# Three score buffers for the prompt's attention units, a place of its own for each value page set, and loads moved between queues, in a two-layer decoder step

## The chip, the cores and the metric

The kernel runs on one core of a Trainium2 chip. A core has five engines with queues of their own: TensorE (PE in the profile, its weight loads are PEld), VectorE (DVE), ScalarE (ACT), GpSimd (POOL) and SyncE (SP). They wait for each other through semaphores only; SP computes nothing here and issues most DMAs, POOL and ACT issue some. The metric is the device time of one execution in microseconds.

## The reference

One inference step of a decoder with two layers, for 256 prompt rows and 8 sequences of 4 new rows each (288 columns together), model width 1024, all float32. Each layer norms the rows, projects them, runs a token mixer beside a cross-attention into 256 memory tokens, projects back, adds, and runs a SwiGLU channel mixer. Layer 0's mixer is a state-space scan; layer 1's is a sparse attention with three branches, each with its own softmax, gated and summed:

```python
def nsa_sample(h, mem_kv, pool_cmp, pool_slc, win_buf, page_table, w_in, ...):
    q, kv_cmp, kv_slc, kv_win, gates, qm = nsa_split(h @ w_in)
    past_cmp = pool_cmp[page_table]...          # 16 pages of 128 rows per sequence
    o_cmp, p = cmp_attend(q, q_pos, ckv, slopes)
    tok = block_tokens(select_blocks(p, q_pos, total))
    kv_past = pool_slc[pages, tok_past % PAGE_SIZE, hi]
    o_slc = slc_attend(q, q_pos, tok, kv_sel, slopes)
    o_win = win_attend(q, q_pos, kv_w, k_pos, slopes)
```

For the 8 sequences, 16 key pages and 16 value pages each come from a pool by a page table; for the prompt, the same branches are computed from the prompt's own rows, for 12 heads.

## The kernel before

Activations lie with features on the partitions, so a projection is a series of 128x128 weight tiles against 288 columns. Weights pass through three slots of a tile called `slabs` (`SLOTS = 3`, 2048 columns each, 1 MB a slab). SP loads slab n when the slab three before it has been used: `load` (L1967) waits for a semaphore and issues. Every engine's program is written out by hand in one order, and a wait blocks all that stands behind it on that engine's queue. PSUM has 8 banks; `banks.fill`, `take`, `give` are the semaphores by which PE writes a bank, a reader takes it and gives it back.

The work in order, on the profile's time axis: layer 0's memory projection, input projection with the memory attention's steps in between (0 to 91 us), the scan with the compression of the cached pages beside it (to 360), output projection and channel mixer (`channel_mixer`, L719 first half with `in_wfi` slabs, L759 second half with `in_wfo` slabs; to 614); layer 1's memory projection (L517), input projection (L497; to 725), the sparse attention (725 to 934), output projection, channel mixer and stores (to 1247).

Places that the change touches:

- Layer 0's start. VectorE makes the scan's input matrices in two rounds r = 0 and 1 (L1631 to L1637: four products and one sum each) and then does `mem_soft(0, 2)`, `(0, 3)`, `(0, 4)`: the softmax of memory heads 2 and 3 and of the sequences, whose results PE turns (L552, L584). SP loads the cached pages of sequence 0 (16 DMAs, L2003), then the second half of the memory values (L2007), which PE multiplies in L596.
- Layer 0's end and layer 1's start. SP issues the 16 `in_wfo` slabs, then 16 key pages (L398, `load_key_pages(sp, SP, 0, 0)`), then layer 1's memory slabs. After the input projection's slabs it also fills the three slots with the first three slabs of layer 1's output projection.
- The units (L972 to L980 on PE, L1821 to L1826 on VectorE). A unit n is one pair of prompt heads in one branch; there are 12. PE makes its scores (L923), VectorE adds the distances (`unit_max`, L1790, L1794, L1795), ScalarE takes the exponential (L1350), VectorE scales (`unit_prob`, L1806, L1808, L1814), PE transposes (L934), ScalarE copies, PE multiplies with the values (L947, L951, L954). The scores of unit n live in `SU[n % 2]`, so `unit_max(n)` waits until unit n - 2 has been transposed. Beside each unit PE computes one tile of the sequences' scores against a key page chunk (`page_scores`, L968, bank 7 alone) and VectorE evicts it (`page_scores_out`, L1799). Four chunks of key pages (c = 0 to 3, 16 pages on SP and 16 on POOL) serve three units each; two places in `arena` alternate, so chunk c waits for the last page scores of chunk c - 2.
- After the units. Window keys and values are loaded and used (L1008, L1040 first part), the selected-block softmax is made, its weights are transposed 16 times (L1061), and then PE multiplies them with the value pages in four pairs of sequences, 32 matmuls on 16 pages each plus 2 (L1040), in order (0,1), (2,3), (4,5), (6,7). A matmul counts twice in the profile's rows (two passes). The value pages (L405) of even sequences are loaded by SP, of odd ones by POOL, in order, each set of 16 when its place is free: 0 and 1 after the window scores, 2 to 4 after the window values' use, 5 and 6 after the transposes (they lie over the scores in `phase`), 7 after the first pair, into the place of sequence 1:

```python
VSLOT = [b if b < 7 else 1 for b in range(B)]
...
if b < 2:
    for h in range(H):
        banks.take(eng, ("sws", h))
elif b < 5:
    eng.wait_ge(win_used, 1)
elif b < 7:
    banks.take(eng, ("st", NPG))
else:
    eng.wait_ge(pair_used, 1)
```

## Time and profile before

| | |
|---|---|
| median of 3 runs | 1255.3 us (1254.72 to 1261.52) |
| the profiled execution's own time | 1248.54 us |
| its span | 1246.8 us |
| PE busy | 1122.9 us (90%) |
| VectorE, ScalarE, GpSimd busy | 371.2, 203.2, 244.1 us |
| granted TensorE clock, mean | 0.945 |
| bytes moved | 185.13 MB, mean 148 GB/s |

The span is divided into 40 slices of 31 us; PE is at nine tenths or more in most of them, except at the start and in slices 23 to 31 (about 720 to 960 us), the sparse attention, where its busy share and its granted clock are lower. A row of the timeline gives start, duration (us), engine, line, operation, tiles and, in brackets, how long the engine had been idle before and what ended that. A row of the chain gives start, duration and what the end was waiting for then.

### The profile page before, as it was taken

What the parts mean: (1) busy time and instruction counts of PE and PEld (TensorE: products, weight loads), DVE (VectorE), ACT (ScalarE), POOL (GpSimd) and SP (SyncE); (2) the same over time, 40 slices, a digit from 0 to 9 for tenths busy, and PEclk for the clock granted to TensorE, in tenths of its full rate; (3) what the DMA queues carried; (4) which work ended last, traced back from release to release, by engine and by line L of the source; (5) the groups of instructions that cost most, each with busy time, mean ns of one, the idle gap of its engine ahead of it and who ended that gap; (6) DMA issues with size and microseconds to landing.
All of it is one profiled execution on the core that took longest, in us unless ns stands there. A gap on an engine that the chain in (4) does not pass through costs nothing. (4 is left out here: it accounts for less than half of the span.)

```text
span 1246.8 us, 16400 instructions
## 1 busy us (share of the span) xinstructions
PE 1122.9 (90%) x6032; PEld 819.0 (66%) x6032; DVE 371.2 (30%) x789; ACT 203.2 (16%) x497; POOL 244.1 (20%) x314
## 2 busy tenths in 40 slices
PE   6879999999989999999899986675669899999996
PEld 5555666666767777777667773333547677777774
DVE  5709767420141111100222125657200411111002
ACT  3220000002230000100032114443201300000000
POOL 0707666620001111110000201304420011111000
PEclk9979999999989999999999977888879899999998
DMA  8455443331415666654522452554632243333431
GB/s 321 189 174 180 143 127 114 101 103 37 166 65 203 221 236 238 276 172 140 190 110 101 148 165 70 153 203 131 186 90 102 93 144 135 135 135 104 138 132 70
DMA packets 59112, 185.13 MB, mean 148 GB/s; under 512 B 8609, under 2 KB 39586, under 8 KB 48418
## 3 DMA queue, kind: packets, MB, share of 16 engines
q1 hardware_dynamic: 52466, 166.33, 38.8%
q0 software_dynamic: 6144, 12.59, 3.5%
q10 hardware_dynamic: 432, 5.24, 1.0%
q8 instruction: 48, 0.79, 0.3%
q14 instruction: 22, 0.18, 0.0%
HBM read 180.35 MB, written 10.02 MB: 153 GB/s over the span
## 5 line engine op out<-in xcount | busy, mean ns | idle before, releaser
L719 PE MATMUL banks<-normed,slabs 128*128 128x288 f32 x1408 | 348.0, 411 | 9.1 <-ACT normed L1141 9.1
L719 PEld LDWEIGHTS banks<-normed,slabs 128*128 128x128 f32 x1408 | 271.1, 193 | 85.8 <-issue 10.0
L759 PE MATMUL banks<-hidden,slabs 128*128 128x288 f32 x704 | 171.2, 406 | 1.4 <-issue 1.4
L695 PE MATMUL banks<-arena,phase 128*128 128x384 f32 x512 | 170.9, 492 | 0.0
L759 PEld LDWEIGHTS banks<-hidden,slabs 128*128 128x128 f32 x704 | 133.6, 190 | 39.0 <-issue 2.3
L695 PEld LDWEIGHTS banks<-arena,phase 128*128 128x128 f32 x512 | 96.5, 191 | 65.0 <-issue 1.1
L1424 POOL TENSOR_TENSOR projected<-projected,rstd 128x288 f32<-128x288 f32 x44 | 35.0, 795 | 446.0 <-ACT projected L1208 446.0
L497 PE MATMUL banks<-normed,slabs 128*128 128x288 f32 (+1 forms) x416 | 107.7, 413 | 1.2 <-ACT normed L1141 1.2
L497 PEld LDWEIGHTS banks<-normed,slabs 128*128 128x128 f32 (+1 forms) x416 | 76.5, 189 | 27.4 <-issue 3.7
L1505 DVE TENSOR_TENSOR normed<-normed 128x288 f32<-128x288 f32 x24 | 11.0, 459 | 199.3 <-ACT normed L1201 199.3
L497 PE MATMUL banks<-mixed,slabs 128*128 128x288 f32 x256 | 64.6, 416 | 1.3 <-DVE mixed L1935 1.3
L1208 ACT ACTIVATE projected<-projected 128x288 f32<-128x288 f32 x44 | 19.5, 443 | 281.4 <-DVE projected L1552 281.4
L1557 DVE TENSOR_TENSOR hidden<-projected,banks 128x288 f32<-128x288 f32 x44 | 20.0, 454 | 138.8 <-PE banks L719 130.1
L497 PEld LDWEIGHTS banks<-mixed,slabs 128*128 128x128 f32 x256 | 49.9, 196 | 15.5 <-issue 1.4
L398 POOL DMA_DIRECT2D arena<-in_slck x64 | 33.4, 522 | 134.2 <-issue 130.0
L1552 DVE TENSOR_TENSOR projected<-banks,rstd 128x288 f32<-128x288 f32 x44 | 20.1, 457 | 127.8 <-PE banks L719 127.7
L1201 ACT ACTIVATE normed<-banks 128x288 f32<-128x288 f32 x32 | 13.2, 411 | 264.1 <-PE banks L759 164.2
L517 PE MATMUL banks<-slabs,mixed 128*128 128x256 f32 x128 | 32.8, 423 | 14.7 <-DMA slabs<-in_w 9.5
L405 POOL DMA_DIRECT2D arena<-in_slcv x48 | 27.9, 581 | 65.9 <-issue 63.1
L517 PEld LDWEIGHTS banks<-slabs,mixed 128*128 128x128 f32 x128 | 27.4, 216 | 19.6 <-issue 15.1
L934 PE MATMUL banks<-cst,hidden 128*128 128x128 f32 x72 | 13.6, 339 | 25.1 <-DVE hidden L1814 25.1
L1461 POOL TENSOR_TENSOR phase_small<-normed,phase 128x512 f32<-128x512 f32 (+1 forms) x15 | 17.1, 1142 | 95.2 <-DVE normed L1696 65.9
(281 smaller groups left out, 1099.8 us busy)
## 6 DMA issues: line engine op xcount, KB each, us to landing
slabs<-in_wfi SPq DMA_DIRECT2D x44, 1024.0 KB, 4.8
slabs<-in_w SPq DMA_DIRECT2D x25, 1024.0 KB, 4.9
arena<-in_cmp SPq DMA_DIRECT2D x128, 192.0 KB, 2.7
slabs<-in_wfo SPq DMA_DIRECT2D x32, 704.0 KB, 4.0
arena<-in_slck POOLq DMA_DIRECT2D x64, 96.0 KB, 2.7
arena<-in_slck SPq DMA_DIRECT2D x64, 96.0 KB, 2.4
out_win_old<-in_winold SPq DMA_DIRECT2D x8, 762.0 KB, 6.3
arena<-in_slcv POOLq DMA_DIRECT2D x48, 96.0 KB, 2.6
```

The source lines that it names most:

```text
L398: eng.dma_start(AR[lo:lo + 64, a:a + 384], page(slck_in, r)).then_inc(kpage_loaded[c % 2][parity], 16)
L405: eng.dma_start(dst, page(slcv_in, r)).then_inc(vpage_loaded[s], 16)
L497: ins = nc.tensor.matmul(BK[b][0:n_out, 0:T], wt[:, k, c * P:c * P + n_out], rhs[:, k, :], start=(k == 0), stop=(k == kc - 1))
L517: ins = nc.tensor.matmul(BK[b][:, 0:256], MEMT[:, k, t * P:t * P + P], wt[:, k, :], start=(k == 0), stop=(k == KC - 1))
L695: ins = nc.tensor.matmul(out.rearrange("p h (g s) -> p h g s", s=8), W1S[:, c, a, j, :], PG[b % 2][:, :, c * 8 + j, :, :].rearrange("p g h ...
L719: return nc.tensor.matmul(BK[2 * (u % SLOTS) + c][:, 0:T], wt[:, k, c * P:c * P + P], Hn[:, k, :], start=(k == 0), stop=(k == KC - 1), ski ...
L759: ins = nc.tensor.matmul(BK[b][:, 0:T], wt[:, k, :], HD[:, 11 * kh + k, :], start=(kh + k == 0), stop=(kh * 11 + k == 21))
L1208: A(z, z, ACT.Silu).then_inc(silu_done, 1)
L1424: tt(z, z, RST[:, :], ALU.mult).then_inc(up_done, 1)
L1461: ch.tick(tt(hr, re, cos, ALU.mult))
L1552: banks.give(tt(z, BK[2 * (u % SLOTS)][:, 0:T], RST[:, :], ALU.mult), key)
L1557: banks.give(tt(HD[:, u, :], z, BK[2 * (u % SLOTS) + 1][:, 0:T], ALU.mult), up)
```

## The change

Three score buffers for the units (the third in a free part of `phase_small`), and VectorE evicts the page scores after `unit_prob`. The value pages of sequences 0 and 1 go into the `slabs` tile, where the output projection's first slabs were preloaded; 2 and 3 take the places of 0 and 1, 4 to 6 those of 2 to 4, 7 that of 5 in `phase`. SP and POOL load the values of 0 and 1 behind key chunk 1. The output projection's slabs are loaded by SP behind the value pages of sequence 6, after the first pair. Key chunk 0 on SP is cut into four pieces that stand between the `in_wfo` slabs. In layer 0 the second half of the memory values is loaded by ScalarE, behind its copies of the scan's input matrices, and `mem_soft(0, 2)` and `(0, 3)` stand between the two rounds of matrices.

```diff
-        SU = [HID[:, 3072 + 768 * r:3840 + 768 * r].rearrange("p (g n) -> p g n", g=2) for r in range(2)]
+        SU = [x.rearrange("p (g n) -> p g n", g=2) for x in (HID[:, 3072:3840], HID[:, 3840:4608], XT[:, C2N:C2N + 768])]
...
-        VAL = [AR[:, a:a + 3072] for a in (6144, 9216, 0, 3072)] + [KV[:, :]] + [U[:, 3072 * s:3072 * s + 3072] for s in range(2)]
-        VSLOT = [b if b < 7 else 1 for b in range(B)]
+        VAL = [W_[:, 0:3072], W_[:, 3072:6144]] + [AR[:, a:a + 3072] for a in (6144, 9216, 0, 3072)] + [KV[:, :], U[:, 0:3072]]
...
             if b < 2:
+                for n in range(FIRST["out", 1] - SLOTS, FIRST["out", 1]):
+                    eng.wait_ge(*released[n])
+            elif b < 4:
                 for h in range(H):
                     banks.take(eng, ("sws", h))
-            elif b < 5:
+            elif b < 7:
                 eng.wait_ge(win_used, 1)
-            elif b < 7:
+            else:
                 banks.take(eng, ("st", NPG))
-            else:
-                eng.wait_ge(pair_used, 1)
...
+            banks.take(act, ("ms", 0, 4))
+            act.dma_start(AR[:, 6144:8192], memv_in[0][:, 2048:4096]).then_inc(mv_loaded[1], 16)
             mem_exp(0, 4)
...
             query_blocks(1, 15)
-            for c in range(1, 4):
+            load_key_pages(pool, POOL, 1, 1)
+            wait_value_slot(pool, 1)
+            load_value_pages(pool, POOL, 1)
+            for c in range(2, 4):
                 load_key_pages(pool, POOL, c, 1)
-            for b in range(1, B, 2):
+            for b in range(3, B, 2):
                 wait_value_slot(pool, b)
                 load_value_pages(pool, POOL, b)
...
                 tt(BX[r], BX[r], BX[2], op).then_inc(bx_done, 1)
                 dve.wait_ge(bx_done, r + 1)
+                if r == 0:
+                    mem_soft(0, 2)
+                    mem_soft(0, 3)
             ch.step(ts(CM[1], CM[1], -1.0, None, ALU.mult))
-            for hd in range(2, 5):
-                mem_soft(0, hd)
+            mem_soft(0, 4)
...
-                s = SU[n % 2]
-                if n >= 2:
+                s = SU[n % 3]
+                if n >= 3:
                     for par in range(2):
-                        banks.take(dve, ("ut", n - 2, par))
+                        banks.take(dve, ("ut", n - 3, par))
...
             for n in range(13):
                 if n < 12:
                     unit_max(n)
-                    page_scores_out(n // H, n % H)
                 if n >= 1:
                     unit_prob(n - 1)
+                if n < 12:
+                    page_scores_out(n // H, n % H)
...
             load_pages(0)
-            banks.take(sp, ("ms", 0, 4))
-            sp.dma_start(AR[:, 6144:8192], memv_in[0][:, 2048:4096]).then_inc(mv_loaded[1], 16)
             store_mem_kv(0)
...
-            load_stage("fo", 0, FO)
-            load_key_pages(sp, SP, 0, 0)
+            for u in range(FO):
+                load(FIRST["fo", 0] + u)
+                if u % 2 == 1 and u < 8:
+                    load_key_pages(sp, SP, 0, 0, [u // 2])
             load_stage("mem", 1, N_MEM_SLAB)
             load_stage("in", 1, N_NSA_SLAB)
-            for s in range(SLOTS):
-                load(FIRST["out", 1] + s)
...
-            for c in range(1, 4):
+            load_key_pages(sp, SP, 1, 0)
+            wait_value_slot(sp, 0)
+            load_value_pages(sp, SP, 0)
+            for c in range(2, 4):
                 load_key_pages(sp, SP, c, 0)
...
-            for b in range(0, B, 2):
+            for b in range(2, B, 2):
                 wait_value_slot(sp, b)
                 load_value_pages(sp, SP, b)
-            load(FIRST["out", 1] + 3)
+            sp.wait_ge(pair_used, 1)
+            load_stage("out", 1, N_OUT_SLAB)
```

On VectorE, unit 2 of the kernel before, with what each row waits for (bank 4 and 5 hold the transposed unit 0, banks 0 and 1 the scores of unit 2, bank 7 the page scores):

```order
L1790 SCALAR_TENSOR_TENSOR hidden<-phase_small,banks 128x384 [waits bank0_full,bank5_full,bank4_full]
L1790 SCALAR_TENSOR_TENSOR hidden<-phase_small,banks 128x384 [waits bank1_full]
L1794 TENSOR_REDUCE stats<-hidden 128x2 [waits bank1_free,bank0_free]
L1795 TENSOR_REDUCE stats<-hidden 128x2 [waits dve_steps]
L1799 SCALAR_TENSOR_TENSOR phase<-phase,phase_small,banks 128x512 [waits bank7_full]
L1806 RECIPROCAL stats<-stats 128x4 [waits unit_exp]
L1808 TENSOR_TENSOR stats<-stats,cmp_hidden 128x4 [waits dve_steps]
L1814 TENSOR_SCALAR hidden<-hidden,stats 128x128 [waits unit_weights]
L1814 TENSOR_SCALAR hidden<-hidden,stats 128x256
L1814 TENSOR_SCALAR hidden<-hidden,stats 128x128
L1814 TENSOR_SCALAR hidden<-hidden,stats 128x256
```

The same place in the kernel after (L1796 is `unit_max`, L1812 to L1820 `unit_prob`, L1805 the page scores' eviction):

```order
L1796 SCALAR_TENSOR_TENSOR phase_small<-phase_small,banks 128x384 [waits bank0_full]
L1796 SCALAR_TENSOR_TENSOR phase_small<-phase_small,banks 128x384 [waits bank1_full]
L1800 TENSOR_REDUCE stats<-phase_small 128x2 [waits bank1_free,bank0_free]
L1801 TENSOR_REDUCE stats<-phase_small 128x2 [waits dve_steps]
L1812 RECIPROCAL stats<-stats 128x4 [waits unit_exp]
L1814 TENSOR_TENSOR stats<-stats,cmp_hidden 128x4 [waits dve_steps]
L1820 TENSOR_SCALAR hidden<-hidden,stats 128x128 [waits unit_weights]
L1820 TENSOR_SCALAR hidden<-hidden,stats 128x256
L1820 TENSOR_SCALAR hidden<-hidden,stats 128x128
L1820 TENSOR_SCALAR hidden<-hidden,stats 128x256
L1805 SCALAR_TENSOR_TENSOR phase<-phase,phase_small,banks 128x512 [waits bank7_full]
```

The wait for banks 5 and 4 before unit 2's first row is gone (the first of this kind is now before unit 3's, for unit 0's transposes), unit 2's scores lie in `phase_small`, and the eviction of the page scores stands behind the scaling of unit 1.

On SP, behind the last value pages that it loads, in the kernel before (the slab is the fourth of the output projection):

```order
L405 DMA phase<-in_slcv 128x192
L402 REGISTER_ALU
L402 COMPARE_AND_BRANCH
L1971 DMA slabs<-in_w 128x2048 [waits bank3_full]
L1971 DMA slabs<-in_wfi 128x2048 [waits bank1_full]
L1971 DMA slabs<-in_wfi 128x2048 [waits bank3_full]
```

The same place in the kernel after:

```order
L403 DMA cmp_kv<-in_slcv 128x192
L400 REGISTER_ALU
L400 COMPARE_AND_BRANCH
L1978 DMA slabs<-in_w 128x2048 [waits bank5_full,pair_values_used]
L1978 DMA slabs<-in_w 128x2048 [waits bank4_full]
L1978 DMA slabs<-in_w 128x2048 [waits bank6_full]
L1978 DMA slabs<-in_w 128x2048 [waits bank3_full]
L1978 DMA slabs<-in_wfi 128x2048 [waits bank1_full]
```

All four slabs of the output projection now stand here, the first behind the wait for the first pair (`pair_values_used`); the pages before them go to `cmp_kv` (sequence 6), not to `phase`.

## Rows read from the trace of the kernel before

**Rows 1.** Chain that ended last, page scores' last tile to output projection.

```profile
828.79 1.04 PE banks L968 x8
...
920.59 8.09 PE banks L1040 x68
...
934.50 33.41 PE banks L497 x128
```

**Rows 2.** Timeline, POOL's value pages for sequences 5 and 7, first of each.

```profile
886.30 2.47 POOL L405 DMA_DIRECT2D phase<-in_slcv  x4 [3.69 <-issue]
...
903.65 2.47 POOL L405 DMA_DIRECT2D arena<-in_slcv  x4 [1.73 <-issue]
```

**Rows 3.** Timeline, PE's first and third pair of value products.

```profile
884.68 5.41 PE L1040 MATMUL banks<-arena,hidden 128*48 128x192 f32 x64 [0.88 <-ACT normed L1304]
...
904.50 0.53 PE L1040 MATMUL banks<-cmp_kv,hidden 128*48 128x192 f32 x1 [8.15 <-DMA phase<-in_slcv]
```

**Rows 4.** Timeline, units on PE and VectorE.

```profile
757.78 1.06 PE L968 MATMUL banks<-arena,phase 128*32 128x512 f32 x8
...
775.92 1.93 PE L968 MATMUL banks<-arena,phase 128*32 128x512 f32 x8
...
785.78 0.87 PE L934 MATMUL banks<-cst,hidden 128*128 128x128 f32 x6 [2.20 <-DVE hidden L1814]
...
786.75 1.02 DVE L1790 SCALAR_TENSOR_TENSOR hidden<-phase_small,banks 128x384 f32<-128x384 f32 x2 [1.02 <-PE banks L934]
...
788.82 1.06 PE L968 MATMUL banks<-arena,phase 128*32 128x512 f32 x8
...
789.95 0.75 DVE L1799 SCALAR_TENSOR_TENSOR phase<-phase,phase_small,banks 128x512 f32<-128x512 f32 x1 [0.94 <-PE banks L968]
...
792.08 1.14 PEld L934 LDWEIGHTS banks<-cst,hidden 128*128 128x128 f32 x6 [3.11 <-DVE hidden L1814]
```

**Rows 5.** Stretches: units, memory values' load; last columns granted clock, DMA share, GB/s.

```profile
756.00:840.00 84.00, 58.09 (x388) 29.46 (x389) 49.76 (x134) 35.08 (x123) 16.66 (x32) 0.84 0.45 151
76.00:82.00 6.00, 3.61 (x58) 2.79 (x50) 1.10 (x4) 2.58 (x7) 0.00 (x0) 1.00 0.95 267
```

**Rows 6.** Timeline, SP's queue: key pages twice, value pages once.

```profile
599.37 15.24 SPq L398 DMA_DIRECT2D arena<-in_slck  x16
...
737.23 70.34 SPq L398 DMA_DIRECT2D arena<-in_slck  x48
...
882.94 15.38 SPq L405 DMA_DIRECT2D cmp_kv<-in_slcv  x16
```

**Rows 7.** Timeline, PE and VectorE at layer 1's start.

```profile
619.86 16.48 PE L517 MATMUL banks<-slabs,mixed 128*128 128x256 f32 x64 [5.18 <-issue]
...
622.41 0.82 DVE L1528 TENSOR_TENSOR residual<-residual,projected 128x288 f32<-128x288 f32 x2
...
638.06 0.53 ACT L1141 ACTIVATE normed<-residual,params 128x288 f32<-128x288 f32 x1
```

**Rows 8.** Waits of SP's queue: us in total, times, longest.

```profile
SPq L1971 <- PE banks L759: 131.6, 26, 5.9
```

**Rows 9.** Timeline, layer 0's memory attention, all engines.

```profile
59.28 0.69 DVE L1537 TENSOR_REDUCE stats<-banks 128x2 f32<-128x512 f32 x1
...
61.93 1.12 PE L552 MATMUL banks<-cst,hidden 128*128 128x128 f32 x4 [5.74 <-DVE hidden L1543]
...
76.91 0.36 SPq L2007 DMA_DIRECT2D arena<-in_memv  x1
...
79.03 0.48 ACT L1167 ACTIVATE hidden<-banks,stats 128x256 f32<-128x256 f32 x1
...
86.29 1.94 PE L596 MATMUL banks<-arena,hidden 128*32 128x128 f32 x32 [4.02 <-DMA arena<-in_memv]
```

**Rows 10.** DMA issues: KB each, median us to landing; key pages' spread.

```profile
slabs<-in_w SPq DMA_DIRECT2D x25, 1024.0 KB, 4.9
...
DMA to landing us min/median/max: 2.2/2.5/4.9
```

More of the change, by code:

```diff
@@ L345, in trunk_kernel @@
         kpage_loaded = [[sem(f"key_pages{s}_{c}_loaded") for c in range(2)] for s in range(2)]
-        vpage_loaded = [sem(f"value_pages{s}_loaded") for s in range(7)]
+        vpage_loaded = [sem(f"value_pages{s}_loaded") for s in range(B)]
         win_used = sem("window_values_used")
@@ L381, in outputs_beside, with load_key_pages @@
             return [OCT - 1, OCT] if blk == OCT else [n for n in (blk,) if n < N_UNIT]
-        def load_key_pages(eng, which, c, parity):
+        def load_key_pages(eng, which, c, parity, pairs=range(4)):
             if c >= 2:
@@ L391, in load_key_pages @@
             lo, base = 64 * parity, 6144 * (1 - c % 2)
-            for b in range(4):
+            for b in pairs:
                 p0 = NPG * (2 * b + parity) + 4 * c
@@ L400, in load_value_pages @@
         def load_value_pages(eng, which, b):
-            s = VSLOT[b]
             with eng.Fori(0, NPG // PG_STEP) as i:
                 for u, r in enumerate(page_numbers(eng, which, b, i, slcv_in)):
-                    dst = VAL[s][:, bass.ds(i * (192 * PG_STEP) + 192 * u, 192)]
-                    eng.dma_start(dst, page(slcv_in, r)).then_inc(vpage_loaded[s], 16)
+                    dst = VAL[b][:, bass.ds(i * (192 * PG_STEP) + 192 * u, 192)]
+                    eng.dma_start(dst, page(slcv_in, r)).then_inc(vpage_loaded[b], 16)
         def wait_value_slot(eng, b):
             if b < 2:
+                for n in range(FIRST["out", 1] - SLOTS, FIRST["out", 1]):
+                    eng.wait_ge(*released[n])
+            elif b < 4:
                 for h in range(H):
                     banks.take(eng, ("sws", h))
-            elif b < 5:
+            elif b < 7:
                 eng.wait_ge(win_used, 1)
-            elif b < 7:
+            else:
                 banks.take(eng, ("st", NPG))
-            else:
-                eng.wait_ge(pair_used, 1)
         released = {}
@@ L933, in unit_turn @@
                     for j in range(3):
-                        ins = nc.tensor.transpose(BK[4 + par][:, P * j:P * j + P], SU[n % 2][:, par, P * j:P * j + P], ident)
+                        ins = nc.tensor.transpose(BK[4 + par][:, P * j:P * j + P], SU[n % 3][:, par, P * j:P * j + P], ident)
                     banks.filled(ins, key)
@@ L1070, in _ @@
                 for c in range(2):
-                    pe.wait_ge(vpage_loaded[VSLOT[b + c]], 16 * NPG * (2 if b + c == 7 else 1))
+                    pe.wait_ge(vpage_loaded[b + c], 16 * NPG)
                 for g in range(NPG):
                     for c in range(2):
-                        ins = seq_pv(b + c, PTS[:, 384 * g:384 * g + 384], VP[VSLOT[b + c]][:, g, :])
+                        ins = seq_pv(b + c, PTS[:, 384 * g:384 * g + 384], VP[b + c][:, g, :])
                 ins.then_inc(pair_used, 1)
@@ L1347, in _ @@
                         for t in range(2):
-                            s = SU[n % 2][:, par, P * t:P * t + P * (t + 1)]
+                            s = SU[n % 3][:, par, P * t:P * t + P * (t + 1)]
                             j = 2 * t + par
@@ L1812, in unit_prob @@
                     for t in range(2):
-                        s = SU[n % 2][:, par, P * t:P * t + P * (t + 1)]
+                        s = SU[n % 3][:, par, P * t:P * t + P * (t + 1)]
                         ins = ts(s, s, w[:, 2 * t + par:2 * t + par + 1], None, ALU.mult)
```

## The prediction

> **What bounds the kernel now.** PE is busy nine tenths of the span, so I first looked on the page for the slices where it is not, then read the chain of waits for who is late there, and last the timeline of each such stretch. Four places came out.
>
> First, the end of the sparse attention. The chain runs from the page scores' last tile through the softmax to the last pair of value products, which starts at 920.59 on POOL's last pages, then to the output projection [rows 1]. PE does the first pair at once, the second behind it, and then sits idle 8.15 us for sequence 5's pages [rows 3] and again until 920.59. What is late is POOL's issuing: sequence 5's sixteen pages start at 886.30, since their place holds the scores until these are transposed, and sequence 7's only behind them, at 903.65 [rows 2]. So 17.35 us of issue stand twice in a row on the path.
>
> Second, the units: PE, VectorE and ScalarE hand one unit round, and none is full. In the unit shown PE starts its transposes at 785.78, VectorE has then been idle 1.02 us when it begins the next unit, waits 0.94 us more for the page scores, and PE waits 2.20 us for the scaling [rows 4]. The granted clock over the stage is 0.84 [rows 5].
>
> Third, layer 1's start: PE stands 5.18 us before the memory projection [rows 7], because SP issues sixteen key pages from 599.37 for 15.24 us, and the projection's slabs only behind them [rows 6].
>
> Fourth, layer 0: PE waits 5.74 us for the softmax of memory head 2, which VectorE begins at 59.28 behind the second round of matrices, and 4.02 us for the second half of the memory values, issued at 76.91 [rows 9].
>
> **The change, part by part.** Times are on the axis of the profiled execution; 1248.54 us is its own time, 1.7 of it outside the span.
>
> *The value pages.* Only sequence 7 is left behind the transposes. POOL's queue then holds 3, 5 and 7, which start when 1, 3 and 5 started before, so sequence 7's pages come when sequence 5's came: PE can begin the last pair at 904.50 [rows 3] instead of 920.59 [rows 1]. PE itself has three pairs from 884.68, each 5.41 us and a short tail (5.8 from pair to pair): 902.1, so the pages still end last. Gain 16.1 us if nothing else moves. Against it: the three slabs that now go out when SP is done with sequence 6's pages (882.94 + 15.38 = 898.3 [rows 6]) share the DMA engines with POOL's last pages. A key page took 2.5 us in the median and 4.9 at most to land [rows 10], so up to 2.4 us later. For it: PE idles 2.4 us before the last pair and not 8, so that pair may run in 5.8 us where it took 8.09 on the lower clock. I take 15, with 10 and 19 as ends. The slabs themselves: 4.9 us each in the median [rows 10]; even one after the other the first lands at 903, the third at 913, while the projection starts some 5.8 us after the last pair's end, at about 918, and needs the third two quarters of 33.41 later [rows 1]. That cover, some 15 us, hides them; without it each microsecond counts in full. Behind SP's new wait for the first pair stand only these slabs and the channel mixer's, and the pair is done at 890, before SP gets there. The values of sequences 0 and 1 stand on SP and POOL behind key chunk 1, where both queues waited for page scores before.
>
> *The units.* With three buffers VectorE need not wait for PE's transposes, and the eviction behind the scaling no longer holds up PE, since PE needs bank 7 only 3.0 us after it starts the transposes (785.78 to 788.82 [rows 4]) and the eviction takes 0.75. What remains: VectorE's own work per unit, 2.26 us of `unit_max` (786.75 to 789.95 less the 0.94 wait), 0.75 of eviction and 1.4 of `unit_prob` (from its end to 792.08) make 4.4, say 4.5 with the semaphores; PE's is 4.1 (785.78 to 789.88) in this unit and some 0.6 less in every other. ScalarE's chain is now beside, not between. Before, a step took (828.79 - 757.78) / 11 = 6.46 us [rows 1, 4]. At the upper clock the eleven steps would gain 21.6. (The two levels are 2.4 and 1.2 GHz.) On the lower one a page score takes 1.93 in place of 1.06 [rows 4]; all of PE's work by that ratio is some 6.9 a unit, PE then sets the step, and eleven steps lose 4.8. A granted clock of 0.84 means a third of the time at the lower level; with that share a quarter of the units are slow, the mean step is 5.1 and the gain 15. The other limit is SP's key chain: chunk 1 from 737.23, then sequence 0's values, chunks 2 and 3, 15.24 + 15.38 + 2 x 15.24 [rows 6], and 2.5 to land, is 800.8; the tenth page score needs chunk 3 and stood at 815.9. So the gain is at most 15 there, and with two quicker steps 19 at the end. PE is denser, so I take 17, ends -5 and 20. Window keys and values are issued behind the page scores as before and move with them.
>
> *Key chunk 0 between the `in_wfo` slabs.* SP waits 131.6 us in 26 waits for PE there, 5.1 each [rows 8]; four pages are a quarter of 15.24, 3.8, and fit into one. If they did not, a slab would come late by the difference, a microsecond or so, four times. The memory slabs then land before PE needs them, and the 5.18 us go. What is late next is nothing until the input projection: VectorE is done with the residual at 623.2, ScalarE's first normed block comes at 638.06, behind its evictions of the memory projection [rows 7], and moves up with PE. Gain 5.2.
>
> *Layer 0.* PE has made head 2's scores before it stands at 56.2, so both softmaxes fit between the rounds and the 5.74 us go [rows 9]. At 2.65 each (59.28 to 61.93) they push the second round's end to about 64.6, before PE comes to its matrices, which is behind the memory scores that SP waited for until 76.91, now 71.2. The memory values' load now stands right ahead of ScalarE's exponential of these scores, at 79.03 [rows 9], so near 73.3 in place of 76.91; its wait is the one that the exponential has anyway. With the same 9.4 us from issue to use PE's wait ends at 82.7, so 3.5 us are gained, not 5.7. Ends 0 and 5.7: the DMA engines are busy 0.95 of the time from 76 to 82 [rows 5]. The Trainium skill ("DMA: Bandwidth & Descriptors", section "Issuing engines are not separate DMA queues") says that DMAs of all queues run on the same 16 engines and that a further queue saves issue time only, usually small beside the transfer. By that rule the move to ScalarE gives nothing where the engines are full, and this term is 0, the sum 37.2. Elsewhere the trace disagrees with "small": sixteen pages cost a queue 15.24 us, one lands in 2.5.
>
> *Sum.* 3.5 + 5.2 + 17 + 15 = 40.7, so 1207.8 for the profiled execution's own time. The median of the runs is 6.8 above that execution; I carry this over: 1255.3 - 40.7 = 1214.6, forecast 1215.
>
> **The rivals.** (a) The units stay mostly at the lower clock: PE's 6.9 sets the step, the stage gains 3 in place of 17, total 26.7, 1229. For it: this stage fell to 0.84 with PE at 58 of 84 us busy [rows 5]. Against: in the unit shown PE stood idle a third of the step, and it will not. (b) The end gains little: sequence 7's pages wait out all three slabs, 898.3 + 3 x 4.9 = 913.0, and the last pair takes 8.6: 921.6 in place of 929, gain 7, total 32.7, 1223. For it, the three slabs are 3 MB at once; against, no key page took more than 4.9. (c) Engines full in layer 0, its term nil: 37.2, 1218. (d) Slower: PE's clock stays at the lower level from the units through the output projection. Units +4.8; four pairs of 8.6 from 884.68 end at 919, 10 less than before; the projection 33.4 more [rows 1]; less 8.7 elsewhere: +20, 1275. It decides once 13 of the projection's 33.4 us run there as well as all before. Against: before, right behind two idle stretches of 8 us, the projection's 128 rows took 0.26 us each [rows 1], as the memory projection's 64 in 16.48 [rows 7]. (e) The change does not do what it says: the step is set elsewhere and POOL's last pages come late by other waits, no difference, 1255.
>
> **How the numbers follow.** Forecast 0.57, (a) 0.20, (b) 0.09, (c) 0.08, (e) 0.02, (d) 0.04. The forecast's own ends (0 + 5.2 + 9 + 13 to 5.7 + 5.2 + 20 + 19) are 27 and 50: 1205 to 1228. With (a) and (b) at their likely sizes and a few microseconds for the runs' own spread, 1201 to 1234. Faster by over 0.5% (6.3 us, about what a measurement here tells from no change) 0.94, within it 0.02, slower 0.04.
>
> **What would show it.** In the profile after: no wait of PE for value pages of sequences 4 and 5, one wait under 5 us before the last pair, one set of POOL pages behind the transposes; page scores 4.5 to 5.3 us apart, VectorE not idle before `unit_max`; the memory projection right behind the channel mixer; no 5.7 us wait in layer 0 and 0 to 4 us for the memory values. Wrong, if PE waits for key chunk 3 by more than 3 us, if a slab of the output projection ends a wait, or if the units' clock falls below 0.8.

## The result and the profile after

The changed kernel runs in 1197.9 us (median of 4 runs, 1197.4 to 1201.0), the kernel before beside it in 1255.0 (4 runs, 1246.9 to 1261.5): a ratio of 0.955, with a 95% interval of 0.950 to 0.961. The forecast was 1215 with a range from 1201 to 1234: faster, as said, but 3 us below the range. The profiled execution after takes 1197.44 us of its own time, with a span of 1195.8 and a granted clock of 0.958, so between the two profiled executions 1248.54 - 1197.44 = 51.1 us went, where the sum said 40.7. Two later runs of the kernel before, of 1263.8 and 1266.8 us at a granted clock of 0.924, count as slow and are left out below.

The four changed stages, as stretches of the trace of before: layer 0 up to its first scan matmul, layer 1 from the residual norm to the input projection, the units with the last two's transposes behind them, and the value pages from the first pair's start to the last pair's. The first number after the stretch is its length, the last three are granted clock, DMA share and GB/s.

```profile
9.48:91.27 81.79, 67.12 (x365) 49.96 (x365) 44.37 (x77) 26.67 (x64) 22.57 (x21) 0.92 0.58 218
...
613.27:638.73 25.46, 18.50 (x73) 14.74 (x72) 7.94 (x17) 4.00 (x10) 0.95 (x1) 0.87 0.52 195
...
757.78:839.39 81.61, 55.97 (x371) 27.78 (x369) 48.79 (x132) 34.59 (x122) 16.66 (x32) 0.84 0.46 155
...
884.68:920.59 35.91, 19.27 (x204) 14.98 (x205) 1.11 (x2) 1.15 (x2) 17.53 (x32) 0.83 0.60 173
```

The same four after, cut at the same instructions:

```profile
8.87:82.78 73.91, 65.88 (x365) 49.03 (x365) 41.46 (x77) 26.64 (x64) 20.50 (x21) 0.95 0.65 245
...
604.32:621.94 17.62, 15.84 (x73) 13.09 (x72) 7.94 (x17) 3.99 (x10) 0.95 (x1) 1.00 0.40 136
...
741.29:801.27 59.98, 48.58 (x370) 23.57 (x369) 47.47 (x132) 34.22 (x122) 16.64 (x32) 0.91 0.60 199
...
846.96:870.15 23.19, 17.45 (x205) 13.58 (x205) 1.11 (x2) 1.14 (x2) 8.74 (x16) 0.93 0.77 251
```

| stage | predicted | measured |
|---|---|---|
| layer 0 | 3.5 | 81.79 - 73.91 = 7.88 |
| layer 1's start | 5.2 | 25.46 - 17.62 = 7.84 |
| units | 17 | 81.61 - 59.98 = 21.63 |
| value pages | 15 | 35.91 - 23.19 = 12.72 |
| everything else | 0 | 1.03 |
| sum | 40.7 | 51.10 |

Look at the granted clock (the third number from the end) and at PE's busy time (the second number). PE has the same work, but is busy for 18.50 us in layer 1's start before and 15.84 after, and 55.97 and 48.58 in the units: the clock is higher.

Layer 0 and layer 1's start after, PE, VectorE and ScalarE's queue, against [rows 7, 9]:

```profile
55.86 0.66 PE L551 MATMUL banks<-cst,hidden 128*128 128x128 f32 x4
...
58.23 0.55 DVE L1637 TENSOR_TENSOR cmp_kv<-phase_small,s_small 128x384 f32<-128x384 f32 x1
...
70.94 0.35 ACTq L1259 DMA_DIRECT2D arena<-in_memv  x1
...
77.80 1.94 PE L595 MATMUL banks<-arena,hidden 128*32 128x128 f32 x32 [3.12 <-DMA arena<-in_memv]
...
605.57 13.98 PE L516 MATMUL banks<-slabs,mixed 128*128 128x256 f32 x64
```

The 5.74 us wait of [rows 9] and the 5.18 us wait of [rows 7] are gone. The memory projection also takes 13.98 us instead of 16.48 [rows 7], and the memory values, issued 6 us earlier, reach PE 6.9 us after their issue instead of 9.4.

The units after, against [rows 4]; the row of `L967` is a tile of page scores:

```profile
753.13 31.42 SPq L397 DMA_DIRECT2D arena<-in_slck  x32
754.51 1.06 PE L967 MATMUL banks<-arena,phase 128*32 128x512 f32 x8
...
755.92 0.88 PE L933 MATMUL banks<-cst,phase_small 128*128 128x128 f32 x6 [0.34 <-DVE phase_small L1820]
...
758.38 1.07 PE L967 MATMUL banks<-arena,phase 128*32 128x512 f32 x8
...
770.34 1.06 PE L967 MATMUL banks<-arena,phase 128*32 128x512 f32 x8 [3.58 <-DMA arena<-in_slck]
771.34 1.39 PE L933 MATMUL banks<-cst,phase_small 128*128 128x128 f32 x6
...
794.09 1.06 PE L967 MATMUL banks<-arena,phase 128*32 128x512 f32 x8
```

PE's wait of 2.20 us for the scaling has shrunk to 0.34 in the unit shown; it is 2.43 for the first unit and at most 1.25 for the others. The page scores run from 741.29 to 794.09, (794.09 - 741.29) / 11 = 4.80 us apart. There is a new wait of 3.58 us at the seventh, for key chunk 2, whose pages and chunk 3's SP issues from 753.13 for 31.42 us; right behind it the transposes take 1.39 us instead of 0.88, and the granted clock from 770.34 to 777.00 is 0.59.

The last pair after, POOL's queue and PE, against [rows 2, 3]:

```profile
848.24 2.47 POOL L403 DMA_DIRECT2D phase<-in_slcv  x4 [2.62 <-issue]
...
858.54 5.41 PE L1039 MATMUL banks<-arena,hidden 128*48 128x192 f32 x64
...
861.47 32.68 SPq L1978 DMA_DIRECT2D slabs<-in_w  x4
...
870.15 0.53 PE L1039 MATMUL banks<-cmp_kv,hidden 128*48 128x192 f32 x1 [5.74 <-DMA phase<-in_slcv]
...
879.15 3.55 PE L1087 MATMUL banks<-cst,normed 48*64 48x16 f32 x48 [1.29 <-issue]
```

The third pair follows without a wait, and one set of pages is left behind the transposes. But PE still waits 5.74 us for it, more than the 5 that the prediction allowed. The first three of the output projection's four slabs are issued from 861.47 on, while POOL is still issuing its last four pages.

### The profile page after: what moved, and what is told of

The parts are those of the page before. It is cut to its first block, busy times and chain, and to the rows that moved or that the text cites. A ratio compares the mean times of both kernels' runs of the same rounds, so it can differ in the third digit from the quotient of the medians.

```text
span 1195.8 us, 16402 instructions
## 1 busy us (share of the span) xinstructions
PE 1109.1 (93%) x6032; PEld 810.3 (68%) x6032; DVE 366.4 (31%) x789; ACT 202.5 (17%) x497; POOL 242.1 (20%) x314
## 4 chain that ended last, share of the span: by engine, by line
PE 87%; DVE 4%; issue 2%; SPq 2%; DMA 2%; ACT 1%; POOLq 0%; POOL 0%; DVEq 0%
PE banks L718 29%; PE banks L496 16%; PE banks L758 14%; PE banks L694 14%; PE banks L516 3%; SPq L397 1%; PE banks L664 1%; PE banks L1039 1%; PE banks L849 1%; PE banks L677 1%; PE banks L562 1%; PE banks L1060 1%; SPq L393 1%; DMA phase<-in_slcv 1%; PE banks L471 1%
## 5 line engine op out<-in xcount | busy, mean ns | idle before, releaser
L1517 DVE RECIPROCAL rstd<-rstd 128x288 f32<-128x288 f32 x8 | 15.6, 1953 | 62.9 <-ACT rstd L1131 62.9
L403 POOL DMA_DIRECT2D arena<-in_slcv x32 | 20.1, 630 | 43.2 <-issue 41.7
```

The costliest lines, as they stand in the source:

```text
L403: eng.dma_start(dst, page(slcv_in, r)).then_inc(vpage_loaded[b], 16)
```

## The experiments

The question was first which edit carries which part of the 51 us, then why three of the four parts came out larger than their waits. The changed kernel was run once more as a yardstick.

> The changed kernel once more, beside the others on one chip: 1197 to 1201 by both theories; its clock in the stretch from the memory projection to the units shows what of the differences between the kernels lies there.

Measured 1197.42 us (1195.7 to 1198.3), so 1197.7, the middle between this and 1197.94, stands below for the changed kernel. The runs below lie on four chips; the kernel before, run beside them on each, took 1248.9 to 1252.3 us in the median, so differences of a few microseconds are read together with the rows of the trace.

**Layer 0, the softmaxes put back.**

```diff
-                if r == 0:
-                    mem_soft(0, 2)
-                    mem_soft(0, 3)
             ch.step(ts(CM[1], CM[1], -1.0, None, ALU.mult))
-            mem_soft(0, 4)
+            for hd in range(2, 5):
+                mem_soft(0, hd)
```

> The changed kernel with the softmaxes of memory heads 2 and 3 put back behind VectorE's second round of matrices; the memory values' load stays on ScalarE. Theory (both edits of layer 0 are needed, one behind the other): PE stands some 5.7 us for head 2 again, the second round runs at 1.4 to 1.6 us an operation again beside GpSimd's sums instead of 0.55, the load is issued near 78 and the first s5_in matmul starts at 89 to 91 instead of 82.78; time 1203 to 1206. Rival 1 (moving the load did it all): first s5_in matmul within 1.5 us of 82.78, time 1197 to 1200. Rival 2 (VectorE and GpSimd do not slow each other, the 0.55 has another cause): the second round stays near 0.55.

Measured 1204.9 us (1203.6 to 1207.7), 7.2 more. GpSimd, VectorE, PE and ScalarE's queue of this kernel:

```profile
45.90 11.56 POOL L1440 TENSOR_TENSOR arena<-arena 128x512 f32<-128x512 f32 x8
...
52.72 1.62 DVE L1638 TENSOR_TENSOR cmp_kv<-phase_small,s_small 128x384 f32<-128x384 f32 x1
...
61.96 1.11 PE L551 MATMUL banks<-cst,hidden 128*128 128x128 f32 x4 [5.94 <-DVE hidden L1547]
62.87 5.13 PE L496 MATMUL banks<-normed,slabs 128*128 128x288 f32 x16
...
78.55 0.35 ACTq L1259 DMA_DIRECT2D arena<-in_memv  x1
...
83.51 1.93 PE L595 MATMUL banks<-arena,hidden 128*32 128x128 f32 x32 [1.21 <-DMA arena<-in_memv]
```

The theory holds in each row, with the scan's first matmul at 88.49, a little before the 89 that was expected. Both rivals fall: the softmaxes' place matters, and beside GpSimd's sums the same product takes 1.62 us where it takes 0.55 once GpSimd is done (58.23 in the changed kernel). Behind its wait PE takes 5.13 us for sixteen rows of the input projection, at a granted clock of 0.74 (61.96 to 68.00), where without the wait it takes 4.05.

**Layer 0, the load back on SP.**

```diff
-            banks.take(act, ("ms", 0, 4))
-            act.dma_start(AR[:, 6144:8192], memv_in[0][:, 2048:4096]).then_inc(mv_loaded[1], 16)
...
             load_pages(0)
+            banks.take(sp, ("ms", 0, 4))
+            sp.dma_start(AR[:, 6144:8192], memv_in[0][:, 2048:4096]).then_inc(mv_loaded[1], 16)
```

> The changed kernel with the second half of layer 0's memory values loaded from SP's queue again, behind the sixteen compressed pages. Theory (the load was late because SP was still issuing pages, and landed late because it was queued behind them): issued near 74.9, 9 us until PE has it, first s5_in matmul at 88 to 90 instead of 82.78, time 1202 to 1205. Rival (a further queue gives nothing where the DMA engines are full): within 1 us of 82.78, time 1197 to 1199.

Measured 1202.3 us (1202.1 to 1202.6), 4.6 more. SP's queue and PE:

```profile
59.38 13.99 SPq L2008 DMA_DIRECT2D arena<-in_cmp  x16
73.59 0.36 SPq L2012 DMA_DIRECT2D arena<-in_memv  x1
...
82.44 1.94 PE L595 MATMUL banks<-arena,hidden 128*32 128x128 f32 x32 [7.67 <-DMA arena<-in_memv]
```

The rival falls, though the scan's first matmul comes at 87.58, a little before the 88 to 90 that was expected. The load goes out when SP has issued its sixteen pages, and reaches PE 8.9 us later, where it took 6.9 from ScalarE's queue.

**Layer 1's start, key chunk 0 in a row again.**

```diff
-            for u in range(FO):
-                load(FIRST["fo", 0] + u)
-                if u % 2 == 1 and u < 8:
-                    load_key_pages(sp, SP, 0, 0, [u // 2])
+            load_stage("fo", 0, FO)
+            load_key_pages(sp, SP, 0, 0)
```

> The changed kernel with key chunk 0's sixteen pages on SP issued in a row behind the eight in_wfo slabs again. Theory (the stage lost its wait and, with it, the lower clock that followed): PE waits about 5.2 us before the memory projection, and the projection takes 16 to 16.5 us instead of 13.98; time 1204 to 1207. Rival (only the wait): the wait is back, the projection stays at 14 us, time 1201 to 1203.5.

Measured 1203.9 us (1201.8 to 1205.3), 6.2 more, between the two expectations in time; the trace decides.

```profile
610.02 15.84 PE L516 MATMUL banks<-slabs,mixed 128*128 128x256 f32 x64 [5.26 <-issue]
```

Wait and slower projection are both back. Whether the one causes the other is asked at the end of this section.

**The units, one edit at a time.** First the third buffer (the three other places that index the buffers change from 3 to 2 as well):

```diff
-                s = SU[n % 3]
-                if n >= 3:
+                s = SU[n % 2]
+                if n >= 2:
                     for par in range(2):
-                        banks.take(dve, ("ut", n - 3, par))
+                        banks.take(dve, ("ut", n - 2, par))
...
```

> The changed kernel with two score buffers for the units, the page scores' eviction still behind the scaling. Theory (the place of the eviction carries the units' gain; with it VectorE finds PE's transposes done but for 0 to 0.3 us a unit): page scores 4.8 to 5.2 us apart, time 1197 to 1201. Rival (the third buffer carries it): page scores 5.6 to 6.5 us apart, time 1206 to 1217.

Measured 1198.3 us (1197.4 to 1198.7): no difference, page scores (795.34 - 741.40) / 11 = 4.90 apart. The third buffer gives the changed kernel nothing. Then the eviction's place:

```diff
                     unit_max(n)
+                    page_scores_out(n // H, n % H)
                 if n >= 1:
                     unit_prob(n - 1)
-                if n < 12:
-                    page_scores_out(n // H, n % H)
```

> The changed kernel with the page scores' eviction put back ahead of the scaling; three score buffers stay. Theory (the place of the eviction alone carries the units' gain): PE waits about 2.2 us for the scaling in every step again, page scores 6.0 to 6.5 us apart, no wait for key pages left, time 1210 to 1217. Rival (the third buffer helps once VectorE may run ahead): page scores 5.0 to 5.6 us apart, time 1199 to 1206.

Measured 1228.2 us (1222.1 to 1232.9), 30.5 more: the mechanism is the theory's, the size beyond both. Two steps of PE, and the clock over the units:

```profile
751.29 1.58 PE L967 MATMUL banks<-arena,phase 128*32 128x512 f32 x8
755.08 0.91 PE L933 MATMUL banks<-cst,hidden 128*128 128x128 f32 x6 [2.21 <-DVE hidden L1820]
760.03 1.93 PE L967 MATMUL banks<-arena,phase 128*32 128x512 f32 x8
```

```profile
741.96:836.95 94.99, 69.30 (x371) 31.20 (x369) 47.88 (x132) 34.51 (x122) 16.72 (x32) 0.66 0.40 134
```

The wait is 2.21 us, as in [rows 4], but the step is 8.74 us, since PE's work runs mostly at the lower level: a page score 1.93 instead of 1.06. With both edits undone (the two diffs together):

> The changed kernel with both unit edits undone: two score buffers, and the eviction ahead of the scaling. It is to be read beside the kernel with the eviction alone put back, which ran 1222.1 to 1232.9 with page scores 7.7 us apart. Theory (PE's 2.2 us wait in each step and the lower clock that goes with it are all there is; the third buffer changes neither): page scores 6.4 to 7.8 us apart, each step 6.3 us at the upper clock and up to 8.7 at the lower, time 1218 to 1232. Rival (with the eviction ahead of the scaling a third buffer does harm): page scores 6.2 to 6.6 apart as in the kernel before, time 1212 to 1217.

Measured 1226.0 us (1220.9 to 1228.7), page scores (817.91 - 740.24) / 11 = 7.06 apart, granted clock 0.76 over the units:

```profile
740.24:827.18 86.94, 61.29 (x370) 28.92 (x368) 48.78 (x132) 34.60 (x122) 16.59 (x32) 0.76 0.45 148
```

The rival falls: a third buffer does no harm that these runs can tell. The two unit edits together are worth 28 us in the changed kernel, all of it, as far as the runs can tell, by the eviction's place. This is more than the 21.6 us of the stage, since the units now take 86.94 us where the same order took 81.61 in the kernel before, at a clock of 0.84. Why the clock is lower here with the same wait of 2.2 us in each step stays open.

**The value pages, back in their old places** (an excerpt; SP and POOL also wait and load in the old order again).

```diff
-        VAL = [W_[:, 0:3072], W_[:, 3072:6144]] + [AR[:, a:a + 3072] for a in (6144, 9216, 0, 3072)] + [KV[:, :], U[:, 0:3072]]
+        VAL = [AR[:, a:a + 3072] for a in (6144, 9216, 0, 3072)] + [KV[:, :]] + [U[:, 3072 * s:3072 * s + 3072] for s in range(2)]
+        VSLOT = [b if b < 7 else 1 for b in range(B)]
...
+            for s in range(SLOTS):
+                load(FIRST["out", 1] + s)
...
-            sp.wait_ge(pair_used, 1)
-            load_stage("out", 1, N_OUT_SLAB)
+            load(FIRST["out", 1] + 3)
```

> The changed kernel with the value pages in their old places and the output projection's slabs loaded early again; units, layer 0 and key chunk 0 stay changed. Theory (issue of two sequences on POOL behind the transposes): POOL starts sequence 5 near 848 and sequence 7 near 865.6, the last pair begins near 882.5 instead of 870.15, the units keep their time; time 1208 to 1213. Rival (the new places gave little of the 51 us, since the slabs now collide with the last pages): time under 1204.

Measured 1211.8 us (1210.8 to 1213.1), 14.1 more. Two waits of PE are back, and the stretch from the first pair to the last is 35.89 us again:

```profile
868.62 0.53 PE L1040 MATMUL banks<-cmp_kv,hidden 128*48 128x192 f32 x1 [7.91 <-DMA phase<-in_slcv]
...
884.95 0.53 PE L1040 MATMUL banks<-phase,hidden 128*48 128x192 f32 x1 [8.62 <-DMA arena<-in_slcv]
```

The rival falls. Undone one by one, units, value pages, key chunk 0 and softmaxes add to 28.3 + 14.1 + 6.2 + 7.2 = 56 (the load lies on one chain with the softmaxes and is not added), near the 54 to 57 that the groups of runs show for the whole. That they meet is in part chance: by the rows of the stages the units are worth 21.6, not 28.3, and layer 0 with its load 7.9.

**The two new waits, taken away.** The slabs of the output projection later:

```diff
-            sp.wait_ge(pair_used, 1)
+            sp.wait_ge(pair_used, 3)
             load_stage("out", 1, N_OUT_SLAB)
```

> The changed kernel with SP's wait ahead of the output projection's slabs for the third pair's values instead of the first's. Theory (the slabs, issued from 861.5, hold up sequence 7's last pages, which reach PE 6.8 us after their issue where it was 1.8 before): the last pair begins at 865 to 866.5 instead of 870.15, the first slab still lands before the projection wants it; time 1193 to 1195. Rival 1 (the last pages are late by POOL's own descriptors): last pair at 869 to 871, time 1197 to 1199. Rival 2 (the slabs are now late): PE waits for a slab at the projection, time 1197 or more.

Measured 1191.9 us (1191.4 to 1194.3), 5.8 less. In the profiled execution the units began 2.9 us later than in the changed kernel's; from the first pair (850.52) to the last it is 18.31 us instead of 23.19. The theory holds, with a median 1 us below its range, and both rivals fall:

```profile
867.56 23.42 SPq L1978 DMA_DIRECT2D slabs<-in_w  x4
...
868.83 0.33 PE L1039 MATMUL banks<-cmp_kv,hidden 128*48 128x192 f32 x1 [0.84 <-DMA phase<-in_slcv]
```

PE's last pair starts at 0.33 us an operation instead of 0.53, so the lower clock is spared too: it is 7.15 us to PE's next step (875.98) at a granted clock of 1.00, where it was 9.00 at 0.79.

Then key chunk 2 in a place of its own (an excerpt; the window keys and values exchange places, and the values of sequences 0 and 1 are loaded behind chunk 2's use):

```diff
-        KP = [AR[:, a:a + 6144].rearrange("p (b g h n) -> p b g h n", b=4, g=4, h=H) for a in (6144, 0)]
+        KAT = [AR[:, 6144:12288], AR[:, 0:6144], W_[:, 0:6144], AR[:, 6144:12288]]
+        KP = [x.rearrange("p (b g h n) -> p b g h n", b=4, g=4, h=H) for x in KAT]
...
-            if c >= 2:
-                banks.take(eng, ("sk", c - 2, H - 1))
+            if c == 3:
+                banks.take(eng, ("sk", 0, H - 1))
+            elif c == 2:
+                for n in range(FIRST["out", 1] - SLOTS, FIRST["out", 1]):
+                    eng.wait_ge(*released[n])
```

> The changed kernel with key chunk 2 loaded into the slabs ahead of the units, chunk 3 into chunk 0's place, window keys and values exchanging places, and the values of sequences 0 and 1 loaded into the slabs behind chunk 2's last page score. Theory (the issue of chunks 2 and 3, 15.7 us each behind the third page score, sets the units' time now): no wait of PE for key pages over 1 us, first to last page score 46 to 48.5 us instead of 52.8, and no lower clock in the middle of the units; time 1190 to 1194. Rival 1 (VectorE or the clock sets the step): 51 to 53 us, time 1197 to 1199. Rival 2 (the values moved behind it come late or meet the window's load): a new wait of PE for window or value pages, time 1197 or more.

Measured 1191.8 us (1189.9 to 1193.1), 5.9 less; page scores (790.19 - 743.77) / 11 = 4.22 apart, no wait for key pages among PE's waits, granted clock 0.97 over the units:

```profile
743.77:797.20 53.43, 45.32 (x370) 22.63 (x368) 47.43 (x132) 34.15 (x122) 17.13 (x32) 0.97 0.60 189
```

Both together:

> Both edits that gained 6 us each, in one kernel: key chunk 2 in the slabs, and the output projection's slabs loaded behind the third pair. Theory (they are in different stages and add): first to last page score 46 to 47 us, last pair 18 to 19 us behind the first, time 1184.5 to 1187.5. Rival (with the units shorter, POOL's last pages or the first output slab end last): a PE wait over 2 us at the last pair or for a slab, time 1188 to 1192.

Measured 1184.1 us (6 runs, 1182.4 to 1187.9), ratio to the kernel before 0.946 (0.942 to 0.950): the fastest version, 13.6 us below the changed kernel. The two gains add up, the rival falls; PE's waits in the attention for DMAs are down to this one:

```profile
PE banks L1042 <- DMA phase<-in_slcv: 0.7, 1, 0.7
```

In this version the third buffer was taken away again (the diff of the two buffers above):

> The kernel with both edits, with two score buffers in place of three. In the changed kernel the third buffer made no difference, while key pages were waited for. Theory (PE's transposes of a unit are done in the time of the eviction, which now stands behind the scaling): the same within 1.5 us as with three, page scores 4.1 to 4.4 us apart. Rival (the key pages hid the buffer's worth): VectorE waits 0.2 to 0.5 us a unit for PE, time 2.5 to 6 us longer than with three.

Measured 1187.0 us (6 runs, 1185.4 to 1195.0), 2.9 more than with three; page scores (791.55 - 741.65) / 11 = 4.54 apart instead of (786.18 - 739.75) / 11 = 4.22. The rival holds: each step costs 0.3 us, and VectorE waits 3.9 us in ten waits for PE's transposes, which the wait for key pages had hidden in the changed kernel. The ranges of the two groups of six runs overlap by 2.5 us, so the size is less sure than the step.

**Does waiting bring the lower clock?** PE is given useless work in its waits, and nothing else is changed. In the units with both edits undone (an excerpt):

```diff
+                banks.fill(pe, ("ut", n, 0), 4)
+                for _ in range(14):
+                    nc.tensor.transpose(BK[4][:, 0:P], ident, ident)
                 pe.wait_ge(u_prob, n + 1)
```

> The changed kernel with both unit edits undone (1220.9 to 1228.7 without more, granted clock 0.76 over the units), and in each step fourteen useless transposes of the identity ahead of PE's wait for the scaling, some 2.05 us at the upper clock, into the bank that the step's transposes then overwrite. Theory (PE's idle 2.2 us in each step bring the lower clock, and that, not the wait itself, is half of the units' price): granted clock over 0.93, page scores 6.2 to 6.5 us apart, time 1212 to 1217, shorter with more work. Rival (the lower clock has another cause): the clock stays at 0.66 to 0.80, the added work takes up to twice as long and comes late, page scores 7 to 9 us apart, time 1222 or more.

Measured 1210.5 us (1209.5 to 1212.4), 15.5 less than without the useless work. A step of PE (`L930` is the useless work), and the stretch of the units:

```profile
777.13 1.06 PE L971 MATMUL banks<-arena,phase 128*32 128x512 f32 x8
778.13 1.75 PE L930 MATMUL banks<-cst 128*128 128x128 f32 x14
780.40 0.87 PE L937 MATMUL banks<-cst,hidden 128*128 128x128 f32 x6 [0.52 <-DVE hidden L1824]
```

```profile
744.45:817.00 72.55, 64.75 (x544) 40.42 (x542) 49.60 (x136) 35.03 (x125) 16.93 (x32) 1.00 0.52 178
```

VectorE's scaling comes as late as ever (1.75 + 0.52 = 2.27 us), but the clock is 1.00 instead of 0.76, and the page scores are (806.65 - 744.45) / 11 = 5.65 apart instead of 7.06. This distance and the time are a little below what the theory expected, and the rival falls. The two kernels ran on different chips, but the kernel before differs by only 2.5 us between these (1251.4 and 1248.9). So the cause is PE's idle time. And in key chunk 0's kernel, 34 such transposes (3.87 us) ahead of the memory projection:

> The kernel with key chunk 0 in a row (1201.8 to 1205.3; PE waited 5.26 us and the memory projection's 64 rows then took 15.84 us), with 34 useless transposes of the identity in that wait, some 5.0 us at the upper clock. Theory (the idle time brings the lower clock): the projection takes 14.0 us behind them, some 1.9 us gained, time 1200 to 1203.5. Rival: the projection stays at 15.5 to 16.5 us, time 1202 to 1206.

```profile
606.99 3.87 PE L514 MATMUL banks<-cst 128*128 128x128 f32 x34
612.37 14.08 PE L523 MATMUL banks<-slabs,mixed 128*128 128x256 f32 x64 [1.51 <-DMA slabs<-in_w]
```

The projection takes 14.08 us instead of 15.84, at a granted clock of 1.00 instead of 0.89. The time, 1205.5 us (1202.6 to 1208.4) against 1203.9, doesn't show the gain: by its expectation it belongs to the rival, while the row is the theory's. In this execution the stage began 2.4 us later (605.73 instead of 603.34), and the 1.8 us of the stage are below what four runs of this spread, on another chip, can tell.

## Why the forecast was right in kind and too small

The stages gained where the prediction said, and the likeliest case was the one that came. Two steps failed.

The first is the carry-over from one execution to the median of the runs. "The median of the runs is 6.8 above that execution; I carry this over": the 6.8 us came from three runs of the kernel before, and no reason was given why the changed kernel should have them. Its median lies 0.5 us above its profiled execution. Without this term the forecast is 1207.8 us and the range 1194 to 1227, which holds the 1197.9 measured. In the groups beside the experiments the kernel before had medians of 1248.9 to 1252.3, 0.3 to 3.7 us above the same execution. Its runs lie on their clock: 1245.3 us at 0.945, 1251.4 at 0.937, 1263.6 at 0.925. The changed kernel's first four runs span 3.6 us, at 0.956 to 0.960. That the spread goes with the waits fits the filled units, where it fell from 8 us to 3, but was not tried apart.

The second is the sum, 40.7 where 51.1 us came. Two of its terms (layer 1's start, layer 0) priced a wait at its own length, while PE's next work behind the wait ran at the lower clock; layer 0's also took the load's way from one queue over to another. The units' term left out the end of the stage, and the value pages' was too large:

- *Layer 1's start*: "Gain 5.2", measured 7.8. The wait was 5.18; the projection's 16.48 us against 13.98 are the other 2.5. The prediction had that number and misread it: in rival (d) it took 0.26 us a row for the upper clock, since the output projection's rows take as much. But those have 288 columns, the memory projection's 256, and the granted clock of this stretch is 0.87.
- *Layer 0*: "3.5 us are gained, not 5.7", measured 7.9. What failed is "the same 9.4 us from issue to use": on ScalarE's queue it was 6.9. The issue came at 70.94 and not at 73.3. It goes out while ScalarE still copies, not when it comes to the exponential, and PE comes 1.5 us earlier than its wait alone gives (4.05 us instead of 5.12 for the next sixteen rows, 0.66 instead of 1.12 for the transposes), which is the clock again. SP was not waiting for the scores until 76.91, as the prediction says: it had issued pages until 62.69 + 14.00 = 76.69. The second round ended at 61.2, not 64.6, since its products no longer ran beside GpSimd's sums.
- *Units*: "I take 17", measured 21.6. The step of 4.80 us lies in the expected 4.5 to 5.3, and the eleven steps give 18.1. Another 3.5 come from the last two units, behind the last page score (10.67 us from 828.72 to 839.39 before, 7.18 from 794.09 to 801.27 after; the granted clock there is 0.70 and 1.00), which the eleven steps left out. The cap by the keys was real, but at the wrong place: not chunk 3 at the end of SP's queue, but chunk 2, which waits for the third page score and then for 15.7 us of issue. "Wrong, if PE waits for key chunk 3 by more than 3 us": it was 0.37 us for chunk 3, 3.58 for chunk 2. Rival (a), the lower clock, did not come: the clock rose from 0.84 to 0.91. The old order with its waits filled takes 71.43 us up to the same place (744.45 to 815.88), at a clock of 1.00, where the kernel before took 81.61. From these two times I estimate that some 10 of the 21.6 us were the clock and the rest PE's waits.
- *Value pages*: "I take 15", measured 12.7 up to the last pair's start. The issue of one sequence did leave the path. Against it, the slabs cost more than "up to 2.4": 4.9 us of landing, as the kernel with later slabs shows. There the last pair also takes 1.9 us less, by the clock; the prediction had counted on that, and it did not come in the changed kernel (9.38 us from the last pair to the next step before, 9.00 after). Rival (b) named this mechanism and priced it at 8 us off the sum; the later slabs give back 5.8.

The range had a weak point that the result did not meet: its lower ends for the units and the value pages, 9 and 13, are not the -5 and 10 that the parts themselves gave.

Rivals (c), (d) and (e) did not happen. On (c), the load on SP costs 4.6 us: 73.59 - 70.94 = 2.65 by its later issue and 2.0 by the longer way from issue to PE. That SP's own pages ahead of it make this way longer is argued from the three times that were measured for this load, not tried apart. By the Trainium skill ("DMA: Bandwidth & Descriptors", section "Issuing engines are not separate DMA queues") the move to another engine's queue saves issue time only. The trace disagrees by the 2.0 us. The same page's section "Queues, rings and completion order" says that each issuing queue has a ring of its own on each DMA engine, and that an engine takes turns between the rings. The rows fit that, but show no ring.

## What to carry to other kernels

Price a wait of PE by its length and by what the following work loses at the lower clock: compare the same instruction, by shape, behind a wait and without one. When such a wait can't be removed, useless work in it can be faster than none, as in the units here; in the memory projection's single wait the time did not show it. And when a step gets shorter, look for the load that is released inside the stage (here chunk 2, by the third page score), not only at the end of the queue. Do not carry the distance between one execution and a median of few runs over to another kernel.

## What was not expected of the hardware

- Useless transposes made the units 15.5 us faster (86.94 us before, 71.43 from 744.45 to 815.88 with them). PE's idle time for the scaling there was only 2.2 us in each step, and yet the granted clock over the units was 0.66 to 0.84 in three kernels; with 0.5 us of it left in each step, it was 1.00.
- One 1 MB load took 8.9 to 9.4 us from its issue to PE behind its own queue's sixteen pages, 6.9 on another queue while these were still being issued, and 5.0 on that queue when the last of them had been issued 3 us before (78.55 to 83.51).
- A product on VectorE took up to 1.62 us beside GpSimd's sums and 0.55 alone. The Trainium skill ("SBUF — State Buffer", section "Who interferes with whom") says that the two engines share a port pair, of which one holder shuts out the other. The longer times fit that; the rows don't show a port.
